# One bias row of a hybrid decoder layer: its products moved from among the weight products to among the zeros at the kernel's start

## The reference, cut to what matters

```
def t5_bucket(dist):
    n = jnp.maximum(dist, 0)
    max_exact = REL_BUCKETS // 2
    ...
    return jnp.where(n < max_exact, n, large)

dist_own = qpos[:, None] - (own * MOBA_BLOCK + j)[None, :]
s_own = jnp.einsum('bhqd,bhjd->bhqj', q_c, k_own) + bias_tab[:, t5_bucket(dist_own)]
s_own = jnp.where(dist_own >= 0, s_own, -jnp.inf)
```

## Time and profile before

| | us |
|---|---|
| median of 3 runs | 687.32 (687.19 to 688.08) |
| the profiled execution | 687.1 |
| its span | 685.3 |
| TensorE busy | 676.4 (99%) |
| VectorE busy | 493.2 (72%) |
| ScalarE busy | 370.3 (54%) |

### The profile page before, as it was taken

One profiled execution on the slowest core, in us unless ns is written; L12 is line 12 of the kernel. 1 busy time (PEld: TensorE's weight loads), 2 busy tenths in 40 slices (PEclk: granted clock), 3 DMA queues, 4 the chain that ended last, 5 costly groups with the idle time before them and its releaser, 6 DMA issues.

```text
span 685.3 us, 11455 instructions
## 1 busy us (share of the span) xinstructions
PE 676.4 (99%) x4521; PEld 618.4 (90%) x4521; DVE 493.2 (72%) x614; ACT 370.3 (54%) x460; POOL 9.9 (1%) x22
## 2 busy tenths in 40 slices
PE   9999999999999999999999999999999999999996
PEld 7999999999999988899888888888898999999995
DVE  5885979696866766777754655556588777777796
ACT  6568867767555544555533433433446555555552
POOL 0000000000100000000000000000000000000001
PEclk9999999999999999999999999999999999999998
DMA  9785768569185457545566666565445555555521
GB/s 298 222 262 185 246 198 251 160 222 332 63 244 195 140 168 230 172 151 179 162 212 222 209 195 183 197 235 173 154 132 189 187 192 180 189 189 183 192 86 62
DMA packets 99505, 130.92 MB, mean 191 GB/s; under 512 B 5649, under 2 KB 73742, under 8 KB 98830
## 3 DMA queue, kind: packets, MB, share of 16 engines
q1 hardware_dynamic: 97926, 125.27, 56.2%
q10 hardware_dynamic: 1544, 5.16, 2.4%
HBM read 129.31 MB, written 2.68 MB: 193 GB/s over the span
## 4 chain that ended last, share of the span: by engine, by line
PE 93%; DVE 3%; ACT 2%; issue 1%; POOL 0%; POOLq 0%; ACTq 0%; DVEq 0%
PE ps L364 29%; PE ps L365 29%; PE ps L366 29%; DVE w_lo L336 2%; PE ps L674 1%; ACT w_hi L332 1%; PE ps L413 1%; PE ps L711 1%; PE ps L675 1%; PE ps L659 1%; PE ps L694 1%; PE ps L419 0%; PE ps L591 0%; ACT h_sc L1222 0%; DVE h_nat L1725 0%
## 5 line engine op out<-in xcount | busy, mean ns | idle before, releaser
L336 DVE TENSOR_TENSOR w_lo<-w_raw,w_hi 128x2048 fp32r<-128x2048 f32 x108 | 247.0, 2288 | 90.4 <-ACT w_hi L332 90.4
L332 ACT ACTIVATE w_hi<-w_raw 128x2048 fp32r<-128x2048 f32 x108 | 206.2, 1910 | 99.0 <-PE ps L366 93.9
L364 PE MATMUL ps<-tok_hi,w_hi 128*128 128x256 f32 x864 | 247.2, 286 | 1.3 <-DVE w_lo L336 1.0
L365 PE MATMUL ps<-tok_lo,w_hi 128*128 128x256 f32 x864 | 244.4, 283 | 0.0
L366 PE MATMUL ps<-tok_hi,w_lo 128*128 128x256 f32 x864 | 244.4, 283 | 0.0
L364 PEld LDWEIGHTS ps<-tok_hi,w_hi 128*128 128x128 f32 x864 | 165.6, 192 | 3.2 <-issue 2.8
L365 PEld LDWEIGHTS ps<-tok_lo,w_hi 128*128 128x128 f32 x864 | 165.7, 192 | 0.4
L366 PEld LDWEIGHTS ps<-tok_hi,w_lo 128*128 128x128 f32 x864 | 165.6, 192 | 0.0
L364 PE MATMUL ps<-w_hi,tok_hi 128*128 128x512 f32 x128 | 50.2, 392 | 0.0
L365 PE MATMUL ps<-w_lo,tok_hi 128*128 128x512 f32 x128 | 49.9, 390 | 0.0
L366 PE MATMUL ps<-w_hi,tok_lo 128*128 128x512 f32 x128 | 49.8, 389 | 0.0
(11 more groups left out here) (264 smaller groups left out, 1000.9 us busy)
## 6 DMA issues: line engine op xcount, KB each, us to landing
w_raw<-w_in SPq DMA_DIRECT2D x94, 512.0 KB, 4.9
w_raw<-w_ffn_up SPq DMA_DIRECT2D x44, 512.0 KB, 4.4
w_raw<-w_ffn_down SPq DMA_DIRECT2D x22, 512.0 KB, 3.9
w_raw<-w_mem_kv SPq DMA_DIRECT2D x16, 512.0 KB, 4.5
w_raw<-w_br_ssm SPq DMA_DIRECT2D x16, 512.0 KB, 4.9
acs_b<-acs_d ACTq DMA_DIRECT2D x4, 1024.0 KB, 6.4
w_raw<-w_br_attn SPq DMA_DIRECT2D x8, 512.0 KB, 4.9
w_raw<-w_br_mem SPq DMA_DIRECT2D x8, 512.0 KB, 4.5
```

Source lines behind the costliest of these rows:

```text
L332: act.activation(w_hi[:, s, :], w_raw[:, s, :], ACT.Copy).then_inc(hi_ready[s], 1)
L336: dve.tensor_tensor(w_lo[:, s, :], w_raw[:, s, :], w_hi[:, s, :].bitcast(F32), ALU.subtract).then_inc(lo_ready[s], 1)
L364: pe.matmul(o, a[0], b[0], start=start, stop=False, **kw)
L365: pe.matmul(o, a[0], b[1], start=False, stop=False, **kw)
```

## The change

The table and the relative bias, with its row of ones, become one array of 33 x 392 on the host, `bias_cols`, and one tile. ScalarE issues its transfer as the first thing in its queue; SP's three are gone. TensorE multiplies 5 zero products into bank 5, waits for the array, makes the three products of the bias row in bank 5, multiplies 8 more zero products into bank 3, opens bank 0 and waits for the copy of the row. VectorE makes that copy, ahead of the diagonals; ScalarE's copy is gone. One zero product less is issued (13 for 14).

```
-            sp.dma_start(table_s[0:BUCKETS + 1, :], table).then_inc(relb_in, 16)
-            sp.dma_start(relb[0:BUCKETS, :], rel_bias).then_inc(relb_in, 16)
-            sp.dma_start(relb[BUCKETS:BUCKETS + 1, :], one_row).then_inc(relb_in, 16)
...
             pe.wait_ge(zeros_set, 1)
-            keep_warm(pe, 14)
+            keep_warm(pe, 5, bank=5)
+            pe.wait_ge(relb_in, 16)
+            for b in range(3):
+                mm = pe.matmul(ps[b * Q:b * Q + HEADS, 5, 0:P], relb[0:BUCKETS + 1, :],
+                               table_s[0:BUCKETS + 1, b * P:(b + 1) * P], start=True, stop=True)
+            mm.then_inc(bias_mm, 1)
+            keep_warm(pe, 8)
             open_bank(pe, 0)
+            pe.wait_ge(bias_copied, 1)
             pe.wait_ge(const_in, 16)
...
             gemm_cols(pe, 0, 1, tok_hi, tok_lo, between=turn_dt)
-            pe.wait_ge(relb_in, 48)
-            for b in range(3):
-                mm = pe.matmul(ps[b * Q:b * Q + HEADS, 5, 0:P], relb[0:BUCKETS + 1, :],
-                               table_s[0:BUCKETS + 1, b * P:(b + 1) * P], start=True, stop=True)
-            mm.then_inc(bias_mm, 1)
             gemm_cols(pe, 0, 2, tok_hi, tok_lo)
...
         def _(act):
+            act.dma_start(bias_s[0:BUCKETS + 1, :], bias_cols).then_inc(relb_in, 16)
             act.wait_ge(small_set, 2)
...
-                    if first and s == 1:
-                        act.wait_ge(bias_mm, 1)
-                        act.activation(bias_row[0:2 * Q + HEADS, :], ps[0:2 * Q + HEADS, 5, 0:P],
-                                       ACT.Copy).then_inc(bias_copied, 1)
...
             dve.memset(wdt_both[:, :, 2 * SHEADS:P].bitcast(F32), 0.0).then_inc(wdt_rest, 1)
+            dve.wait_ge(bias_mm, 1)
+            dve.tensor_copy(bias_row[0:2 * Q + HEADS, :], ps[0:2 * Q + HEADS, 5, 0:P]).then_inc(bias_copied, 1)
             dve.wait_ge(const_in, 16)
```

More of the change, by code:

```diff
@@ L101, in constants, with build @@
     table[BUCKETS] = np.where(dist < 0, np.float32(MASKED), np.float32(0))
-    return square, table, np.ones((1, HEADS), np.float32)
-def build(nc, x, mem, rel_bias, w_in, b_gate, w_mem_kv, w_br_attn, w_br_ssm, w_br_mem, w_out, w_ffn_up, w_ffn_down,
-          final_norm_g, square, table, one_row, mem_cols, mix_cols, columns, out):
+    return square, table
+def build(nc, x, mem, w_in, b_gate, w_mem_kv, w_br_attn, w_br_ssm, w_br_mem, w_out, w_ffn_up, w_ffn_down,
+          final_norm_g, square, bias_cols, mem_cols, mix_cols, columns, out):
     base = -(-nc.sbuf_base // 64) * 64
@@ L123, in build @@
     cb_mask = sq[:, P:4 * P]
-    table_s = place("table_s", 90.5, [BIAS_W])
-    relb = place("relb", 92, [HEADS])
+    bias_s = place("bias_s", 90.5, [BIAS_W + HEADS])
+    table_s, relb = bias_s[:, 0:BIAS_W], bias_s[:, BIAS_W:]
     widths = ((TAPS + 1) * CONV_T, 2 * KT + SSM // P, SSM // P, 4 * 2 * FT, 2 * SHEADS)
@@ L407, in open_bank, with keep_warm @@
                   start=True, stop=False, skip_group_check=True)
-    def keep_warm(pe, n):
+    def keep_warm(pe, n, bank=3):
         z = zero_s[:].bitcast(mybir.dt.bfloat16)
         for _ in range(n):
-            pe.matmul(ps[:, 3, :].rearrange("p (a n) -> p a n", n=P), z, z.unsqueeze(1).to_broadcast([P, 4, P]),
+            pe.matmul(ps[:, bank, :].rearrange("p (a n) -> p a n", n=P), z, z.unsqueeze(1).to_broadcast([P, 4, P]),
                       start=True, stop=True)
@@ L1814 @@
     arrays = {n: np.ascontiguousarray(inputs[n]) for n in _INS}
-    arrays |= dict(zip(("square_table", "bucket_table", "one_row"), constants()))
+    arrays["square_table"], table = constants()
+    rel_rows = np.concatenate([arrays.pop("rel_bias"), np.ones((1, HEADS), np.float32)])
+    arrays["bias_cols"] = np.concatenate([table, rel_rows], axis=1)
     arrays["mem_cols"] = np.ascontiguousarray(inputs["mem"][0].T)
```

## The result

The changed kernel takes 688.88 us (22 runs, 687.34 to 689.90) against 687.24 for the kernel before (22 runs, median of the same comparison): a ratio of 1.002, interval 1.0014 to 1.0026, or +1.63 us. That is outside the range of 686.7 to 688.1. The loss is sure; whether it is over the 0.2% (1.37 us) of the prediction is not, since the interval of the ratio reaches down to 0.14%. It is also a wider spread: the middle half of its runs lies between 688.5 and 689.1.

The account below looks back on a forecast made before the run. TensorE, busy 676.4 of 685.3 us, was taken as the bound from about 9.5 us on. Products gone at 25 us, -0.33, plus start cost, +0.17, gave -0.16 us: 687.16 against the median 687.32, range 686.7 to 688.1.

Parts of the forecast that it names:

- the 0.2% (1.37 us) of the prediction: Whole kernel: the change in time that a measurement can tell from none; slower by more was given 6%.
- Term one: At 25 us: taking the three bias products, six passes, out of TensorE's queue gains 0.33 us.
- The copy and SP's queue: ScalarE's bias-row copy and SP's wait and issues, taken away from their old places, were counted as worth nothing.
- if what follows can come earlier: Behind the products: first-group convolution output ends at 41.8, its transposes start at 44.14, 2.4 us in hand, so 0.33 holds.
- The landing: At the start: the array lands at 3.35 us, ends 3.3 and 4.6, leaving TensorE idle for 0.25 us.
- The held-up x: At the start: 52 KB ahead of the due transfers delays them by 0.17 us, bounds 0 and 0.25.
- The forecast itself: Whole kernel: gain at 25 us less start cost, -0.16 us, 687.16 against the median; chance 58%.
- the rival I gave 8%: Among the starting zeros: the gap and narrow products delay the clock's rise, +0.8 to +2.1 us, 688.1 to 689.4; 8%.
- term two: First 10 us: what the start costs with the products in it, 0.17 us, the larger of two parallel delays.
- Zeros then run at 0.427 until 5.50: Zeros behind the products: clock still rises at 5.50, the last zero ends at 6.49, first transpose at 6.8.
- the signs named: Proof of error: first weight product after 10 us, transposes over 0.2 us apart, or a new split wait behind 25 us.
- the "against": Against a late clock rise: gap 0.25 us of 4.5, and sparse work from 6.5 to 9.5 us didn't lower the clock.

Follow-up runs that it names:

- the kernel with seven zeros ahead: Changed kernel with 7 zero products ahead of the bias products and 6 behind, for 5 and 8: 687.40 us, +0.16 against the kernel before.
- stop and narrow products: Kernel before with a TensorE stop after the fifth zero, then three narrow products of zeros and 8 zeros; no array on ScalarE's queue: 689.26 us, +2.02.
- the idle-slot kernel: Kernel before, 14 unbroken zeros, products where TensorE waits for the first token column, joined array on SP's queue after the first weight tile: 687.72 us, +0.48.
- the load alone: Kernel before with the joined array issued first on ScalarE's queue; 14 unbroken zeros, products and copy at their old places: 687.76 us, +0.52.
- a late stop: Kernel before with a 0.75 us TensorE stop after the ninth zero and 4 zeros behind it: 689.12 us against 687.07, ratio 1.0020.
- the last idle-slot kernels: Kernel before, products where TensorE waits for the first token column, array on ScalarE's queue or in SP's middle: 687.25 and 687.20 us against 687.34.
- the product-free kernel: Kernel before without the three bias products, so the bias is left out: 686.88 us against 687.34, ratio 0.9999.
- the kernel with the array in SP's middle: Kernel before, products where TensorE waits for the first token column, array on SP's queue after two weight pieces: 687.20 us against 687.34.

## Why the prediction was wrong

**Term one was mis-sized, too small.** The step "on the chain the six take 0.33 us" counted the passes and not the 0.2 us by which the weight product behind them is longer. Taken out they give 0.51 us. The copy and SP's queue cost nothing, as said. The check "if what follows can come earlier" looked at the convolution output of the first group, with 2.4 us in hand. That of the second had some 0.3: it ends at 82.73 in the kernel before, and its transposes start at 83.04. In seven profiles this is where TensorE waits.

**The landing was mis-sized.** I took 3.35 us and gave 3.3 to 4.6 as the ends. TensorE went on at 3.79 in one profile and 4.21 in the other: a stop of 0.49 or 0.91 us for 0.25. "A tenth of the x tile beside it" was no reason: the array needed 3.0 to 3.4 us from its issue although its queue was empty. Both landings lie inside the ends given.

**The held-up x was mis-sized.** The step "52 / 380 = 0.14 us; I take 0.17, bounds 0 and 0.25" priced bytes at the rate of a busy stretch. Measured: 0.67 us on x, +0.52 us on the kernel with only the load moved. With term one as forecast that makes +0.2, with term one as measured 0.0; the kernel with seven zeros ahead measures +0.16, and its interval holds both. This error alone keeps the time inside the range.

**The forecast itself fell to the rival I gave 8%.** The step that failed is in term two: "Zeros then run at 0.427 until 5.50 (3.4 of them), the other 4.6 at 0.216". It took the moment of the rise from one profile of unbroken zeros and kept it for broken ones. Measured, the clock rose at 7.57 and at 9.34, no zero behind the products but the last ran faster than 0.427, and the first transpose came at 7.86 and 8.56 for the 6.8 forecast. Two of the signs named came true: the first product with a weight after 10 us (10.67), and transposes over 0.2 us apart (0.21 in the slower profile). The rival named the place, the mechanism and +0.8 to +2.1 us; measured, +1.63. What held it at 8% was the "against": that the sparse work between 6.5 and 9.5 us, with a gap of 0.3, did not bring the clock down. Those rows are of a clock that was up already. The change touches the stretch in which it has yet to come up, and there 0.57 us of stop and 0.54 of narrow products made +2.0 us of a kernel that was otherwise unchanged. I also set the gap against the 4.5 us of zeros alone and did not ask what gap and narrow passes do together: alone they cost 0.50 and 0.13 us.

A small reading beside it: the 0.31 of the two weight loads in rows 4 is their busy time; the 0.215 of a quick zero comes from starts (5.58, and 6.01 for the bank opener's load, two zeros on).

Stop and held-up x do not add. The start waits for the later of the zeros and x, so in the changed kernel it is 2.02 (stop and narrow products) - 0.51 = 1.5, near the measured 1.63, and the transfer's 0.5 is hidden behind it. Take the stop away and the transfer is what is left.

The Trainium skill (TensorE: Matmul & The Clock Gate, "What's actually happening") says that the number of matmuls at the lower clock varies from run to run of one kernel. I cited that and gave it a few tenths. The profiles here agree, though each is of another kernel: where 14 zeros run unbroken the rise came in the seventh (3.82 us, the idle-slot kernel), in the eleventh (5.49, before), or with the last (6.95, the load alone). Fourteen zeros from 0.99 end at 6.97 even when none is quick. By an estimate from these rows the first transpose of the kernel before would then come at about 7.2 for 6.51, and of the 0.7 us some 0.25 is covered: by this estimate a late rise costs it half a microsecond at most. That would be why its runs lie close together. The changed kernel's zeros end near 7.8 or later when none is quick, and its runs spread over 2.6 us; that the one follows from the other was not tested.

## What to carry to other kernels

Products that keep TensorE busy until its clock rises are not free space: a wait put among them, with narrow products or a longer one alone, cost about twice its own length here (1.1 us of either made 2.0 to 2.3), and a late stop 0.3 us in some runs and 2.1 in others. So fill such a stretch only behind work that has surely landed, or leave it unbroken and use an idle place after the rise. A small transfer issued together with the large one that everything waits for is priced by what it does to that one's landing, measured, not by its bytes over the bandwidth. Where runs of a kernel fall into two groups, one profile shows one of them: look at the times before believing its rows. And before a saving is counted, look for every later place where the next engine is barely in time, not only for the first.

## What the runs showed that I had not expected

A stop of 0.57 us alone cost 0.50 us, narrow products alone 0.13, together 2.02. A transfer of 52 KB, issued together with the first half of 1 MB on another queue, cost that half 0.67 us, one of 1 KB nothing to speak of (4.21 for 4.12).

Some single executions are 1.2 to 2.3 us slow for another reason, in the kernel before too (four of 33 runs beside the last idle-slot kernels lie at 688.53 to 689.62). The profile of the product-free kernel caught one, at 688.62: the identity landed 5.4 us after its issue for 3.7 before, and both diagonals waited for it.

```profile
7.50 0.48 DVE L1276 TENSOR_SCALAR diag<-square_c,stat 128x128 f32<-128x128 f32 x2 [5.84 <-DMA square_c<-square_table]
```

The identity is 64 KB, issued fourth, and the whole start hangs on it as much as on x. The first weight tile was late in the same profile (its split starts at 8.40 for 6.88), so not the identity alone. The profile of the kernel with the array in SP's middle, at 688.48, shows the same: 5.2 us for the identity, the split at 8.22. What makes them late is not shown.
